# Half of the adaLN half units summed over their chunks by VectorE instead of TensorE

## The reference

```python
cond = jax.nn.silu(c)                       # (1, 1024)
for l in range(2):
    mod = cond @ w_ada[l] + b_ada[l]        # w_ada[l] is (1024, 6144): 24 MB
    sh1, sc1, g1, sh2, sc2, g2 = split(mod, 6)
    h = rms_norm(x) * (1 + sc1) + sh1
    ... = split_columns(h @ w_in[l])        # GLA q k v a r, window attention q k v, mix gates a b
    y_gla = gla_branch(...) @ w_up_gla[l];  y_swa = swa_branch(...) @ w_up_swa[l]
    merged = sigmoid(mix_a) * y_gla + sigmoid(mix_b) * y_swa
    x = x + g1 * (merged @ w_out[l])
    h2 = rms_norm(x) * (1 + sc2) + sh2
    x = x + g2 * moe_ffn(h2)                # 16 experts, two of them for each token
```

## Time and profile before

| | us |
|---|---|
| median of 3 runs | 1470.93 (1466.42 to 1476.77) |
| profiled execution, its own time | 1472.26 |
| span of its instructions | 1470.1 |
| TensorE busy | 1365.5 (93%) |
| VectorE busy | 973.1 (66%) |
| ScalarE busy | 722.5 (49%) |
| share of TensorE in the chain that ended last | 74% |

### The profile page before, as it was taken

How to read it: one execution, slowest core, us unless ns; L and a number is a source line. 1 busy time by engine, 2 the same in 40 slices (tenths; PEclk the granted TensorE clock), 3 DMA queues, 4 the chain that set the end, 5 groups by cost and what they waited for, 6 DMA issues and landing times.

```text
span 1470.1 us, 18679 instructions
## 1 busy us (share of the span) xinstructions
PE 1365.5 (93%) x7011; PEld 1082.0 (74%) x7012; DVE 973.1 (66%) x948; ACT 722.5 (49%) x768; POOL 305.9 (21%) x263
## 2 busy tenths in 40 slices
PE   3999999999999999999949999999999999999793
PEld 1766776666777888888748787788788788888572
DVE  4226476223668999999981558642648899999284
ACT  4334355122246777776642536513325777776270
POOL 1000000000125345445220000000023444445130
PEclk9999989999999999999979999999999999999997
DMA  9766501776578999999842230131456999999365
GB/s 300 266 215 208 193 1 72 242 249 240 185 266 302 359 379 386 391 377 376 301 136 83 89 116 0 72 105 68 143 200 223 334 373 375 378 378 382 117 257 191
DMA packets 157544, 342.95 MB, mean 233 GB/s; under 512 B 16998, under 2 KB 19258, under 8 KB 157474
## 3 DMA queue, kind: packets, MB, share of 16 engines
q1 hardware_dynamic: 141170, 316.97, 59.6%
q0 software_dynamic: 16304, 25.05, 4.9%
HBM read 351.73 MB, written 23.63 MB: 255 GB/s over the span
## 4 chain that ended last, share of the span: by engine, by line
PE 74%; DMA 8%; DVE 8%; ACT 3%; DVEq 3%; issue 2%; SPq 1%; POOL 0%; ACTq 0%; POOLq 0%
PE PS L1195 15%; PE PS L1197 14%; PE PS L1196 14%; PE PS L1603 7%; PE PS L1607 6%; PE PS L1599 6%; PE PS L1134 3%; DVE ring_parts L2216 2%; DMA ring<-in_w_ada 2%; DMA ring<-in_w_up 2%; DMA ring<-in_w_down 2%; PE PS L1587 1%; ACT reg L956 1%; DMA y_rows<-reg,icur 1%; SPq L485 1%
## 5 line engine op out<-in xcount | busy, mean ns | idle before, releaser
L1195 PE MATMUL PS<-ring_parts 128*128 128x512 f32 (+1 forms) x704 | 278.8, 396 | 11.0 <-DVE hT_parts L1841 5.8
L2216 DVE TENSOR_TENSOR ring_parts<-ring,reg_parts 128x2048 fp32r<-128x2048 f32 x124 | 278.1, 2284 | 3.9 <-ACT reg_parts L1058 3.9
L1058 ACT ACTIVATE reg_parts<-ring 128x2048 fp32r<-128x2048 f32 x124 | 230.4, 1909 | 64.7 <-DMA ring<-in_w_down 38.8
L1833 DVE TENSOR_TENSOR ring_parts<-ring,ring_parts 128x2048 fp32r<-128x2048 f32 (+1 forms) x52 | 112.9, 2210 | 156.2 <-ACT ring_parts L883 156.2
L1195 PEld LDWEIGHTS PS<-ring_parts 128*128 128x128 f32 x704 | 134.7, 191 | 64.8 <-issue 28.5
L883 ACT ACTIVATE ring_parts<-ring 128x2048 fp32r<-128x2048 f32 (+1 forms) x52 | 93.3, 1845 | 157.7 <-DMA ring<-in_w_in 113.6
L2216 DVE TENSOR_TENSOR ring_parts<-ring,hT_parts 128x2048 fp32r<-128x2048 f32 x68 | 155.1, 2286 | 16.8 <-issue 15.1
L1196 PE MATMUL PS<-hT_parts,ring_parts 128*128 128x512 f32 x384 | 150.3, 392 | 0.0
L1197 PE MATMUL PS<-ring_parts 128*128 128x512 f32 x384 | 150.3, 391 | 0.0
L1058 ACT ACTIVATE hT_parts<-ring 128x2048 fp32r<-128x2048 f32 x68 | 126.5, 1909 | 26.2 <-DMA ring<-in_w_gate 19.9
L1607 PE MATMUL PS<-ring_parts,reg_parts 128*128 128x512 f32 x528 | 130.6, 389 | 0.0
(11 more groups left out here) (322 smaller groups left out, 2371.5 us busy)
## 6 DMA issues: line engine op xcount, KB each, us to landing
ring<-in_w_up SPq DMA_DIRECT2D x32, 2048.0 KB
ring<-in_w_gate SPq DMA_DIRECT2D x32, 2048.0 KB, 12.5
ring<-in_w_down SPq DMA_DIRECT2D x32, 2048.0 KB
ring<-in_w_ada SPq DMA_DIRECT2D x40, 1024.0 KB, 5.3
ring<-in_w_in SPq DMA_DIRECT2D x16, 2048.0 KB, 7.8
ring<-in_w_ada SPq DMA_DIRECT2D x4, 2048.0 KB, 12.9
ring<-in_w_out SPq DMA_DIRECT2D x4, 2048.0 KB, 9.9
reg<-y_rows SPq DMA_DIRECT2D x16, 512.0 KB, 6.3
```

The costliest lines, as they stand in the source:

```text
L1058: act.activation(high[:, cols], ring[:, 3 * k + part, cols], ACT.Copy).then_inc(w_hi[part], 1)
L1195: pe.matmul(out_, left[0], right[0], start=first, stop=False)
L1833: tt(ring_r[:, unit_slot(n), cols], w, ring_r[:, 2 + n % 2, cols].bitcast(F32), ALU.subtract).then_inc(lo_done, 1)
L2216: tt(ring_r[:, 3 * k + part, cols], ring[:, 3 * k + part, cols], high[:, cols].bitcast(F32), ALU.subtract).then_inc(w_lo[part], 1)
```

## The change

Eight own halves (0 to 7, four units) and twelve next halves (0 to 3 and 6 to 13, six units) move from TensorE to VectorE. For one of them VectorE does four instructions of 128x512: each takes a chunk of the half times the condition's column (one number for each partition) and adds it to the unit's sum in SBUF; the first of a unit, a `tensor_scalar`, only multiplies, and the other seven are `scalar_tensor_tensor`. A `drain` stands between them. TensorE then multiplies each unit's sum by a window of `ones_at`, which sums the partitions into row u of a quarter: `summed_rows`, four products at own half 9, four after the seventh `W_MB` product and two after the last `W_UPS` product. The other 20 halves stay on TensorE, some at other places: own halves 8 to 11 follow the four `W_QK` products, 12 to 15 are among the `W_R` products; next halves 4 and 5 stand among `W_UPG`'s, 14 to 19 among `W_UPS`'s. A load now waits on whichever engine reads the half before it in its place.

```diff
-    IN_HALVES = (2, 4, 4, 4, 2)
-    MIX_HALVES = (4, 4, 4, 4, 4, 0, 0)
+    IN_HALVES = (2, 4, 2, 4, 4)
+    MIX_HALVES = (2, 4, 4, 4, 6, 0, 0)
+    OWN_SUMMED, NEXT_SUMMED = (*range(8),), (*range(4), *range(6, 14))
...
+        def half_read(number):
+            mine = summed_on_vector(number)
+            count = sum(summed_on_vector(i) == mine for i in range(number + 1))
+            return (ada_summed, count) if mine else (ada_used, ADA_FIRST + count)
...
-                sp.wait_ge(ada_used, ADA_FIRST + max(number - 1, 0))
+                    read, value = half_read(number - 2)
+                    sp.wait_ge(read, value)
...
+            def summed_rows(l, first, last):
+                halves, sums = (OWN_SUMMED, own_sums) if l == 0 else (NEXT_SUMMED, next_sums)
+                read, value = half_read(first_half(l) + halves[2 * last - 1])
+                pe.wait_ge(read, value)
+                for i in range(first, last):
+                    g, u = i % 4, (ADA_FIRST if l == 0 else 0) + halves[2 * i] // 2
+                    pe.matmul(PS[32 * g:32 * g + 32, IN_ADA_BANK if l == 0 else MIX_ADA_BANK, :], ones_at[:, COND_AT - u:COND_AT - u + 32], sums[i],
+                              start=False, stop=False, skip_group_check=True)
...
-                    own_half(10 + m)
+                    own_half(8 + m)
+                    if m == 1 and l == 0:
+                        summed_rows(0, 0, 4)
...
-                    if h < 2:
-                        own_half(14 + h)
+                    for j in ((12,), (13, 14), (15,), ())[h]:
+                        own_half(j)
...
-                    next_half(8 + j)
+                    if j == 6 and l < DEPTH - 1:
+                        summed_rows(l + 1, 0, 4)
...
+            def sum_half(l, j):
+                number, halves, sums = first_half(l) + j, *((OWN_SUMMED, own_sums) if l == 0 else (NEXT_SUMMED, next_sums))
+                weights_, total, h = ada_half(number), sums[halves.index(j) // 2], j % 2
+                dve.wait_ge(ada_loaded[number % 2], 16 * (number // 2 + 1))
+                for g in range(4):
+                    factor = condw[:, 4 * h + g, COND_AT:COND_AT + 1]
+                    if h == 0 and g == 0:
+                        added = ts(total, weights_[:, g, :], factor, None, ALU.mult)
+                    else:
+                        dve.drain()
+                        added = stt(total, weights_[:, g, :], factor, total, ALU.mult, ALU.add)
+                added.then_inc(ada_summed, 1)
...
                 if l == 0:
                     split_low(1)
+                sum_own(0, 1)
                 split_low(2)
+                sum_own(2, 3, 4, 5)
...
                 split_low(3)
+                sum_own(6, 7)
...
                 split_low(W_UPG)
+                if l < DEPTH - 1:
+                    dve.wait_ge(mx_sig, at(mx_sig, l, C // 2))
+                sum_next(0, 1, 2, 3)
...
+                sum_next(6, 7)
                 split_low(W_MB1)
+                sum_next(8, 9, 10, 11)
                 split_low(W_UPS)
+                sum_next(12, 13)
                 split_low(W_O0)
```

More of the change, by code:

```diff
@@ L155, in trunk @@
         cst = sb("cst", [P, 4])
+        ones_at = sb("ones_at", [P, COND_AT + 32])
         warm = sb("warm", [P, 1])
@@ L179, in trunk @@
         scanm = reg5[:, 2 * SEQ:3 * SEQ]
+        own_sums = [reg4[:, 512 * i:512 * i + 512] for i in range(4)]
+        next_sums = [r_[:, 512 * i:512 * i + 512] for r_, n in ((reg5, 4), (reg4, 2)) for i in range(n)]
         rt = reg5[:, 0:20 * NT * E].rearrange("p (a n) -> p a n", n=NT * E)
@@ L273, in trunk @@
         ada_used = sem("ada_weights_used")
+        ada_summed = sem("ada_half_units_summed_by_vector")
         ada_rowed = sem("ada_rows_copied")
@@ L428, in chosen_rows, with layer_and_half, summed_on_vector @@
             return y_rows[2 * P * t:2 * P * (t + 1), :].rearrange("(p k) d -> p k d", k=TOPK)[:, k, :]
+        def layer_and_half(number):
+            return (0, number) if number < first_half(1) else (1 + (number - first_half(1)) // (2 * ADA), (number - first_half(1)) % (2 * ADA))
+        def summed_on_vector(number):
+            l, j = layer_and_half(number)
+            return j in (OWN_SUMMED if l == 0 else NEXT_SUMMED)
+        def half_read(number):
+            mine = summed_on_vector(number)
+            count = sum(summed_on_vector(i) == mine for i in range(number + 1))
+            return (ada_summed, count) if mine else (ada_used, ADA_FIRST + count)
         def halves_used(l):
-            return ADA_FIRST + first_half(l + 1)
+            return half_read(first_half(l + 1) - 1)[1]
         block = ctx.enter_context(nc.Block())
@@ L466, in load_ada_half @@
             def load_ada_half(number):
-                l, j = (0, number) if number < first_half(1) else (1 + (number - first_half(1)) // (2 * ADA), (number - first_half(1)) % (2 * ADA))
+                l, j = layer_and_half(number)
                 u, h = (ADA_FIRST if l == 0 else 0) + j // 2, j % 2
-                sp.wait_ge(ada_used, ADA_FIRST + max(number - 1, 0))
+                if number < 2:
+                    sp.wait_ge(ada_used, ADA_FIRST)
+                else:
+                    read, value = half_read(number - 2)
+                    sp.wait_ge(read, value)
                 sp.dma_start(ada_half(number), w_ada[l, 4 * P * h:4 * P * h + 4 * P, 512 * u:512 * u + 512].rearrange(
@@ L1142, in condition_half, with first_on_tensor @@
                 condition_products(IN_ADA_BANK if l == 0 else MIX_ADA_BANK, ada_half(number), ADA - units + j // 2, j % 2,
-                                   j == 0, j == 2 * units - 1).then_inc(ada_used, 1)
+                                   j == first_on_tensor(l), j == 2 * units - 1).then_inc(ada_used, 1)
+            def first_on_tensor(l):
+                return min(j for j in range(2 * ADA) if j not in (OWN_SUMMED if l == 0 else NEXT_SUMMED))
+            def summed_rows(l, first, last):
[6 more added lines that the diff above has]
+                              start=False, stop=False, skip_group_check=True)
             def condition_columns(bank, group):
@@ L1482, in _ @@
                     channel_major(mix_bank(Q_UPG + j), W_UPG, slice(j * P, j * P + P), rs_parts).then_inc(mx_ready, 1)
-                    if j % 2 == 1:
-                        next_half(4 + j // 2)
+                    if j % 4 == 3:
+                        next_half(4 + j // 4)
                 for j in range(C):
@@ L1501, in _ @@
                     channel_major(mix_bank(Q_UPS + j), W_UPS, slice(j * P, j * P + P), os_parts).then_inc(mx_ready, 1)
-                    if j % 2 == 1:
-                        next_half(16 + j // 2)
+                    if 1 <= j < 7:
+                        next_half(13 + j)
+                    elif j == 7 and l < DEPTH - 1:
+                        summed_rows(l + 1, 4, 6)
                 def router_tokens_half(t, h):
@@ L1731, in _ @@
             dve.memset(condw[:, :, :], 0.0)
+            dve.memset(ones_at[:, :], 0.0)
             dve.memset(cst[:, 0:1], EPS)
@@ L1736, in _ @@
             dve.wait_ge(const_loaded, 16 * 9)
+            dve.drain()
+            dve.memset(ones_at[:, COND_AT:COND_AT + 1], 1.0)
             pf = rt[:, 0, 0:NT]
@@ L1825, in _, with sum_own, sum_next @@
                     second_scale()
+                def sum_own(*halves):
+                    if l == 0:
+                        for j in halves:
+                            sum_half(0, j)
+                def sum_next(*halves):
+                    if l < DEPTH - 1:
+                        for j in halves:
+                            sum_half(l + 1, j)
                 def split_low(n, l=l, parts_=(0, 1)):
```

9 lines of the change are left out of this document (1 added, 8 removed).

## The result

The changed kernel takes 1476.24 us (median of 20 runs, 1471.8 to 1479.47); the kernel before, in 20 runs beside it, 1469.1 (1466.23 to 1476.77). The ratio of all these runs is 1.0038 with an interval of 1.0025 to 1.0052: 5.6 us more, where 2.7 less were forecast. The time lies in the forecast's range and within 1%, but the sign is wrong.

A forecast was written before the change was run, and what follows sets the result against it. TensorE, busy 93% of the span, was taken as the bound, with late loads next. Input stage +3.8, mix stage -8.2 and one clock fall +1.7 gave -2.7 us: 1468.3 us, range 1457 to 1480.

The forecast's parts named there:

- `W_QK` late behind the halves that VectorE reads: Input stage: `W_QK` requested at 91.0 behind half 6, ready at 114.7, so TensorE waits 9 us.
- small waits for loads of `w_ada`: Mix stage: TensorE waits 2 us for half 4 in `W_UPG` and 2 us for half 15 in `W_UPS`.
- What leaves TensorE: Both stages: 1.2 us per half, 24.0 us for 20, less 3.4 for three groups of ones products.
- Rival 2: VectorE's instruction on 512 columns takes 1.285 + 0.08 us by halved throughput and bounds the kernel: 1480.5 us, chance 0.10.
- the wait of 0.9 for half 8: Input stage behind the first `W_QK` tile: half 8 lands at 122.8, while that tile is done at 121.9.
- the 3.8 of the forecast: Input stage as a whole: ends at 175.5, 3.8 us later than before, with ends of +1.5 to +5.5.
- -8.2 + 1.7 = -6.5: Mix stage: 8.2 us shorter, plus 1.7 us for one fall of the clock behind a wait.
- half 4, which could be requested only at 82.5 and lands at 87.6: Input stage: half 4's load, summed until 90.6, holds half 6 and puts the `W_QK` request at 91.0.
- the 2.3 us that the forecast kept of 9.6: Input stage: first `W_QK` product at 114.7 in place of 117.0, out of 8 x 1.2 us saved.
- -12 x 1.2 + 2.2 + 4 = -8.2: Mix stage: twelve halves removed, two groups of ones products added, two waits of 2 us added.
- lands near 348.4: Mix stage, `W_UPS`: half 15, requested behind `W_O0`, is wanted at 346.3, so TensorE waits 2 us.
- the mix stage's ends as -12.2 to -3: Mix stage's forecast range: -12.2 us with no wait, to about -3.

The follow-up runs named there:

- `six_own`: Changed kernel with only own halves 0 to 5 on VectorE, all next halves on TensorE, `W_QK` requested behind half 4: 1465.29 us, ratio 0.9976.
- `own_only`: Changed kernel with only its eight own halves on VectorE, next halves on TensorE as before the change: 1475.3 us, ratio 1.0034 to the kernel before.
- `next_only`: Changed kernel with only its twelve next halves on VectorE, own halves as before the change: 1469.39 us, ratio 0.9999 to the kernel before.
- `one_instruction`: Changed kernel with three of four chunks of each VectorE half left out, loads and order unchanged; other tokens are routed, so its total can't be compared.
- `weights_first`: Changed kernel requesting `W_V` before halves 2 to 5, `W_QK` before 6 to 8, `W_R` before 9; half 6 summed before the squares: 1465.98 us, ratio 0.9963.
- `wqk_ahead_of_half_6`: Changed kernel with one request moved: `W_QK` right behind half 5, ahead of halves 6, 7 and 8: 1467.95 us, ratio 0.9992 to the kernel before.
- `next_retimed`: `next_only` with TensorE's next halves 4, 5 and 14 to 19 at later places, halves 19 and 20 requested behind `W_O1`: 1461.82 us, ratio 0.9944.
- `mix_retimed`: Changed kernel with its input stage kept and its mix stage retimed as in `next_retimed`: 1468.18 us, ratio 0.9996 to the kernel before.
- `twenty_reordered`: Changed kernel's 20 halves, with the input stage of `weights_first` and the retimed mix stage: 1456.12 us, ratio 0.9905 to the kernel before.
- `both_retimed`: `six_own`'s input stage joined with `next_retimed`'s mix stage, 18 halves on VectorE: 1450.29 us, ratio 0.9879 to the kernel before.

## Why the prediction was wrong

**Right.** The mechanism in both stages: `W_QK` late behind the halves that VectorE reads, and small waits for loads of `w_ada`. What leaves TensorE: `six_own` got 6.1 us where 7.2 - 1.0 were due. A VectorE instruction: 0.75 us, 0.82 from start to start, as taken. Its two sources are float32 in SBUF, for which the Trainium skill, "Vector Engine (DVE) Microarchitecture Reference", section "Points that are easy to get wrong", has halved throughput. The trace shows no halving against the `tensor_tensor`: from 512 to 1024 columns the time grows from 0.751 to 1.285 us, 1.04 ns for a column, and so does the `tensor_tensor` from 512 to 2048 (0.68 to 2.28). Rival 2, which hung on it, was not there. `W_V` landed at 73.2 (forecast 73.1) and was split at 79.6 (79.5); TensorE was through with `W_V` at 105.3 (105.4); from `W_QK`'s landing to its readiness 13.8 us (13.8).

From the first `W_QK` product to the attention it took 61.2 us (60.8), and that was luck: the wait of 0.9 for half 8 did not come, and the slow clock cost 3.0 in place of 1.7.

**Where the sign was lost.** By the ratios the input stage alone came out at +5.0 us (`own_only`, 1.8 to 8.2), which holds the 3.8 of the forecast; the mix stage alone at -0.1 (`next_only`, -2.8 to +2.6), where -8.2 + 1.7 = -6.5 were forecast. So it was the mix stage that turned the sign.

**The step that failed in the input stage** is "half 4, which could be requested only at 82.5 and lands at 87.6", priced with the 5.1 us of a half alone. It was requested at 82.6 and took 6.4. That put the request of `W_QK` at 92.4 in place of 91.0, and its split's end, with 0.3 more for its own landing, at 116.5 in place of 114.7. The first `W_QK` product came at 116.6: of the 2.3 us that the forecast kept of 9.6, 0.4 were left. With 0.4 more behind it, the stage came out at +6.0, not +3.8, above my upper end of +5.5.

This is the account of one execution. In the trace of `own_only`, whose input stage is the same, half 4 took 5.2 us and `W_QK` was requested at 90.5:

```profile
81.87 5.17 DMA ring<-in_w_ada
90.48 10.51 DMA ring<-in_w_in
```

That is 36.9 us after the stage's start, and 36.8 were forecast. Yet the first `W_QK` product came 61.3 us after the start, as late as in `next_only` (61.4), and the wait was 11.5 us. In neither trace had the clock fallen at the start. In the kernel before it had, and the 117.0 that the forecast starts from contains that fall, which TensorE paid for there and which the wait for `W_QK` hides in the changed kernel. So where the clock doesn't fall at the start nothing is gained at `W_QK`, even with half 4 on time, and the stage is 6.3 us longer than `next_only`'s. Half 4's delay is 1.3 us of the changed kernel's trace, and not what makes the loss: that is the wait, which in both traces follows a request of `W_QK` some 9 us behind its release (an estimate: TensorE was through with `W_V` at 105.3 and 103.3, four tiles of 5.5 us after that release).

**The step that failed in the mix stage** is the sum -12 x 1.2 + 2.2 + 4 = -8.2, and of it the 4, the two waits, with the 1.7 for one fall of the clock. Half 4 waited 3.0 us, not 2. Half 15 waited 4.1, not 2, and half 14, not in the forecast, 0.6: half 15 "lands near 348.4" in the times of before, which is 350.7 with the 2.3 us by which the stage starts later, and landed at 356.3. VectorE's split of `W_UPS`, forecast for 333 (335.3 in these times), ended at 339.9, because VectorE had stood still for half 11, whose load took 11.4 us behind `W_UPS`:

```profile
332.28 3.23 DVE L1829 SCALAR_TENSOR_TENSOR reg<-ring,condw,reg 128x512 f32<-128x512 f32 x4 [6.50 <-DMA ring<-in_w_ada]
335.43 4.49 DVE L1895 TENSOR_TENSOR ring_parts<-ring,ring_parts 128x2048 fp32r<-128x2048 f32 x2
```

The sums of halves 12 and 13 came behind it, the request at 346.1, and the load took 10.2 us behind `W_O0`. To that come the falls of the clock: I had one, 1.7 us; there were two, of 3.4 and 6.8 us, and 3.4 and 5.2 of them lay behind the wait, so half of 8.6 is 4.3. -12.2 + 7.7 + 4.3 = -0.2; the trace has -0.4.

This form of the sum holds in all the kernels whose mix stage has the twelve halves on VectorE (but `one_instruction`, whose sums are shorter). The length is from the first `W_MA1` product to the router's first transposition, 170.49 us before; "slow" is the low clock behind the waits.

| kernel | length | measured | waits | half of slow | -12.2 + both |
|---|---|---|---|---|---|
| changed kernel | 170.14 | -0.4 | 7.7 | 4.3 | -0.2 |
| `weights_first` | 169.71 | -0.8 | 7.0 | 4.6 | -0.6 |
| `next_only` | 168.37 | -2.1 | 8.3 | 1.7 | -2.2 |
| `wqk_ahead_of_half_6` | 168.04 | -2.5 | 7.0 | 2.9 | -2.3 |
| `next_retimed` | 161.27 | -9.2 | 2.8 | 0 | -9.4 |
| `mix_retimed` | 160.26 | -10.2 | 1.8 | 0 | -10.4 |
| `twenty_reordered` | 159.54 | -11.0 | 1.1 | 0 | -11.1 |
| `both_retimed` | 159.29 | -11.2 | 0.9 | 0 | -11.3 |

So the term for TensorE's work was right to 0.2 us. What I mis-sized were waits and clock: +3.7 and +2.6 in the mix stage, +2.2 in the input stage. With -2.7 that makes +5.8, and the ratio has +5.6. The closeness is owed in part to this one trace, as `own_only` shows.

**Where the chances were wrong.** I gave the mix stage's ends as -12.2 to -3, though each of its waits hung on a chain of VectorE sums and two or three queued megabytes that I had no row for. A wait that is the small difference of two long chains is uncertain by as much as it is long, upwards too; an honest upper end of the mix stage would have been about 0, and "slower" would have stood beside "faster" as a case of its own, near +6.

**Open.** Half 4 took 6.4 us, with nothing queued ahead of it in its own queue, in the changed kernel and in `mix_retimed`, and 5.2 in `own_only` with the same input stage. What makes the difference was not tried. Nor was what decides whether the clock falls at a wait, and how long it stays low.

## What to carry over

Work that is moved to an idle engine can delay what is requested behind it. If the moved work frees a buffer, look at the requests in that queue, and move the big load that the busy engine needs ahead of the one that waits for the slower reader; one such swap was worth 6.8 us by the ratios here, of which the traces show 2 to 3 in the input stage itself. Then put the products that stay on the busy engine where their loads have landed, and move fewer if a wait is left: 18 halves in the right places gave 17.8 us, 20 in the first places cost 5.6. A wait of some 3 us or more on a busy TensorE can cost more than its length: where the clock is low behind it, half of that time is lost again. Behind the mix stage's waits of up to 2.6 us it was not.

## What the runs showed of the hardware

- **The clock behind a wait.** In the three kernels whose wait for `W_QK` was 11.1 to 11.5 us the clock was low for 13.7 us in all, some 6 of them behind the restart. Around the wait of 6.9 us and behind it, it was low twice, for 6.8 us each. At the wait of 5.1 us (`one_instruction`) it was low for 3.4. At waits of 2.9 to 3.5 us it was low for 3.4, or not at all (3.0 us, in `wqk_ahead_of_half_6`); at those of 4.0 and 4.1 for 3.4 or 6.8. At the mix stage's waits of 2.6 us and less it did not fall, but at the start of the input stage, behind the same wait of 2.2 us in all twelve traces, it was low for 3.4 us in four of them and in the other eight not at all. So the length of a wait did not settle it. The same attention stage took 64.7 us without a fall and 68.5 with 10.2 us of low clock in it, so a single trace of this kernel can stand several microseconds off for this alone.
- **Loads behind one another.** In the changed kernel's input stage a half requested 2.9 us behind a two-megabyte weight took 9.9 to 11.2 us, one without a weight right ahead of it 5.1 to 6.4; the weights `W_V` and `W_QK`, 0.4 us behind a half, 10.1 and 10.3.
